# Column tiles side by side for the gate's low-rank product and for two routers' logits

## The reference, cut to what matters

```python
# block 1, mixer: the decay of gated linear attention comes from a product of rank 16
proj = n @ w_in                                   # glr is 16 of its columns
log_a = jax.nn.log_sigmoid((glr @ gla_gate_w2 + gla_gate_b).astype(jnp.float32)) / GLA_TAU   # (16, 256)
# block 1, router: 4 groups and 32 experts, 36 logits per token
g_logits = (x @ w_grp).astype(jnp.float32) + b_grp.astype(jnp.float32)
e_logits = ((x @ w_exp).astype(jnp.float32) + b_exp.astype(jnp.float32)).reshape(M, N_GROUPS, EXPERTS_PER_GROUP)
# block 2, router: each of 16 experts chooses 128 of the 1024 tokens by a softmax over 16 logits per token
```

## Time and profile before

| what | us |
|---|---|
| median of 3 runs (lowest, highest) | 3929.72 (3928.16, 3930.3) |
| span of the profiled execution, first to last instruction | 3925.4 |
| PE busy | 3703.1 (94%) |
| DVE busy | 2843.7 (72%) |
| ACT busy | 1858.2 (47%) |
| mean granted TensorE clock | 0.976 |

### The profile page before, as it was taken

How to read it: one execution, slowest core, us unless ns; L and a number is a source line. 1 busy time by engine, 2 the same in 40 slices (tenths; PEclk the granted TensorE clock), 3 DMA queues, 4 the chain that set the end, 5 groups by cost and what they waited for, 6 DMA issues and landing times. The chain is left out here.

```text
span 3925.4 us, 42186 instructions
## 1 busy us (share of the span) xinstructions
PE 3703.1 (94%) x16780; PEld 2848.1 (73%) x16780; DVE 2843.7 (72%) x2581; ACT 1858.2 (47%) x1720; POOL 264.7 (7%) x281
## 2 busy tenths in 40 slices
PE   8999998899999799999999989899499999999998
PEld 3557776788888677777887634578288888888886
DVE  2655455898988665556345899954799898888887
ACT  3243431778777334443011111211377777777776
POOL 0000000100000200000000000000000101010110
PEclk9999999899999899999999999999799999999999
DMA  3012024899998632223344515143699999999998
GB/s 119 6 51 83 17 93 188 317 419 415 415 415 335 241 116 68 68 67 104 95 123 151 201 56 187 54 161 129 225 373 386 382 389 382 388 381 389 385 385 318
DMA packets 367168, 891.04 MB, mean 227 GB/s; under 512 B 21994, under 2 KB 118609, under 8 KB 357556
## 3 DMA queue, kind: packets, MB, share of 16 engines
q1 hardware_dynamic: 323796, 758.12, 52.0%
q0 software_dynamic: 26896, 97.17, 7.0%
q10 hardware_dynamic: 16336, 33.82, 2.2%
HBM read 788.65 MB, written 100.40 MB: 226 GB/s over the span
## 5 line engine op out<-in xcount | busy, mean ns | idle before, releaser
L2346 DVE TENSOR_TENSOR moe_w_rest<-moe_w_w,moe_upper 128x2048 fp32r<-128x2048 f32 x384 | 862.3, 2288 | 131.9 <-ACT moe_upper L2255 70.7
L2247 ACT ACTIVATE moe_upper<-moe_w_w 128x2048 fp32r<-128x2048 f32 x192 | 357.4, 1909 | 225.0 <-PE moe_y_ps L2211 117.0
L2346 DVE TENSOR_TENSOR moe_w_rest<-moe_w_w,moe_upper_w 128x2048 fp32r<-128x2048 f32 x192 | 430.5, 2283 | 10.9 <-ACT moe_upper_w L2265 10.8
L2265 ACT ACTIVATE moe_upper_w<-moe_w_w 128x2048 fp32r<-128x2048 f32 x192 | 357.5, 1910 | 111.6 <-PE moe_up_ps L2185 81.3
L2255 ACT ACTIVATE moe_upper<-moe_w_w 128x2048 fp32r<-128x2048 f32 x192 | 356.7, 1911 | 0.2
L2185 PE MATMUL moe_up_ps<-moe_upper,moe_x_upper 128*128 128x512 f32 x768 | 308.4, 402 | 0.0
L2185 PE MATMUL moe_gate_ps<-moe_upper,moe_x_upper 128*128 128x512 f32 x768 | 300.8, 392 | 4.7 <-DVE moe_x_rest L2359 4.7
L2185 PE MATMUL moe_gate_ps<-moe_upper,moe_x_rest 128*128 128x512 f32 x768 | 300.3, 391 | 0.0
L2185 PE MATMUL moe_gate_ps<-moe_w_rest,moe_x_upper 128*128 128x512 f32 x768 | 300.1, 391 | 0.0
L2185 PE MATMUL moe_up_ps<-moe_upper,moe_x_rest 128*128 128x512 f32 x768 | 299.9, 390 | 0.0
L2185 PE MATMUL moe_up_ps<-moe_w_rest,moe_x_upper 128*128 128x512 f32 x768 | 298.9, 389 | 0.0
(11 more groups left out here) (636 smaller groups left out, 7512.2 us busy)
## 6 DMA issues: line engine op xcount, KB each, us to landing
moe_w_w<-in_expert_w_dram SPq DMA_DIRECT2D x96, 2048.0 KB, 10.8
moe_w_w<-in_w_gate_dram SPq DMA_DIRECT2D x64, 2048.0 KB, 10.8
moe_w_w<-in_w_up_dram SPq DMA_DIRECT2D x64, 2048.0 KB, 10.3
moe_w_w<-in_w_down_dram SPq DMA_DIRECT2D x64, 2048.0 KB, 10.3
tmp_y_rows<-moe_y ACTq DMA_DIRECT2D x32, 512.0 KB, 9.5
block_w_first<-in_w_in_dram SPq DMA_DIRECT2D x20, 512.0 KB, 3.8
tmp_h<-out_xn POOLq DMA_DIRECT2D x16, 512.0 KB, 3.0
tmp_spectra<-held_K ACTq DMA_DIRECT2D x8, 1024.0 KB, 4.7
```

What stands on the lines that cost most here:

```text
L2247: act.activation(half(upper1(c), h), half(weights.w1[c % 2], h), ACT.Copy).then_inc(m.w1_rounded, 1)
L2265: act.activation(half(upper2(i, c), h), half(weights.w2[c % 2], h), ACT.Copy).then_inc(m.w2_rounded, 1)
L2346: dve.tensor_tensor(half(rest, h), half(whole, h), half(upper, h).bitcast(F32), ALU.subtract).then_inc(done, 1)
```

## The change

1. The weights of each of the three products are padded with zeros to 32, 64 or 32 columns, and the 8 slices of the contraction are dealt to 4, 2 or 4 column tiles of TensorE. Matmuls of different slices write different partitions of one PSUM bank; each column tile accumulates its own 2 or 4 slices.
2. The partial sums are not added by an operation of their own. For the gate, `w2` is loaded 8 times, one copy below the other (7 DMAs more), so that "z" contracts over 128 rows where it contracted over 16 and sums as it multiplies. For the routers the transposes become matmuls with a small matrix of zeros and ones (`sums`, made from the identity by one DVE reduction), which turn and add at once.
3. The first half of the gate's product is computed after the fifth and sixth transpose (4 matmuls each), no longer in four parts.
4. The routers' logits are computed in three parts, tiles 0 to 3, 4 to 6 and 7 (`LOGIT_TILES`). In the first router part 0 stays ahead of the last transpose; in the second, parts 0 and 1 do. ACT copies what was made there between its last square root and its last tile copy.

```diff
+LOW_WIDTH = 2 * GLA_LOW
+LOW_SIDE = P // LOW_WIDTH
...
-        sp.dma_start(m.w2[:, :], m.gate_w2).then_inc(m.loaded["small"], 16)
+        for rows in range(P // GLA_LOW):
+            sp.dma_start(m.w2[bass.ts(rows, GLA_LOW), :], m.gate_w2).then_inc(m.loaded["small"], 16)
...
+    def pad_low(m, dve):
+        dve.memset(m.wlow[:, :, GLA_LOW:LOW_WIDTH], 0.0)
...
-        per = 2 * ND // NT
-        for k in range(per * part, per * (part + 1)):
-            last = m.nc.tensor.matmul(m.low_ps[0:GLA_LOW, 0, :], m.wlow[:, k, :], n_T[:, k, 0:BANK], start=(k == 0), stop=(k == ND - 1))
+        if part < ND // LOW_SIDE:
+            last = m.low_products(m.low_ps[:, 0, :], n_T, 0, part)
...
+    def low_products(m, out, n_T, h, r):
+        for g in range(LOW_SIDE):
+            k = r * LOW_SIDE + g
+            last = m.nc.tensor.matmul(out[bass.ts(g, LOW_WIDTH), :], m.wlow[:, k, :], n_T[:, k, bass.ts(h, BANK)],
+                                      start=(r == 0), stop=(r == ND // LOW_SIDE - 1))
...
+    def prepare(m, dve, ident):
+        dve.memset(m.w[:, :, m.n:m.width], 0.0)
+        dve.reduce_sum(m.sums[:, :], ident[:, :].rearrange("p (g n) -> p n g", n=m.width), axis=AXX)
+
+LOGIT_TILES = ((0, NT // 2), (NT // 2, NT - 1), (NT - 1, NT))
...
+def logit_parts(nc, pe, m, inputs, h_T, normed, part):
+    first_tile, last_tile = LOGIT_TILES[part]
+    cols = slice(first_tile * P, last_tile * P)
+    if part == 0:
+        pe.wait_ge(inputs.loaded, inputs.all_loaded)
+    pe.wait_ge(normed.copied, last_tile)
+    n_side = P // inputs.width
+    for r in range(ND // n_side):
+        for g in range(n_side):
+            k = r * n_side + g
+            last = nc.tensor.matmul(m.logit_T_ps[bass.ts(g, inputs.width), part, 0:(last_tile - first_tile) * P], inputs.w[:, k, :], h_T[:, k, cols],
+                                    start=(r == 0), stop=(r == ND // n_side - 1))
+    last.then_inc(m.logit_T_made, 1)
+
+def sum_logits(nc, pe, m, inputs, out, part):
+    pe.wait_ge(m.logit_T_copied, part + 1)
+    for t in range(*LOGIT_TILES[part]):
+        last = nc.tensor.matmul(out[:, t, :], m.logit_T[:, bass.ts(t, P)], inputs.sums[:, 0:inputs.n], start=True, stop=True)
...
-        router_logits(nc, pe, m, h_T, w, logit_ps, ident, logits_ready, [1])
+        logit_parts(nc, pe, m, inputs, h_T, normed, 1)
+        sum_logits(nc, pe, m, inputs, logit_ps, 0)
+        logit_parts(nc, pe, m, inputs, h_T, normed, 2)
+        for part in (1, 2):
+            last = sum_logits(nc, pe, m, inputs, logit_ps, part)
...
-        router_logits(nc, pe, m, h_T, w, logit_ps, ident, logits_ready, [1])
+        for part in (0, 1):
+            sum_logits(nc, pe, m, inputs, logit_ps, part)
+        logit_parts(nc, pe, m, inputs, h_T, normed, 2)
+        sum_logits(nc, pe, m, inputs, logit_ps, 2).then_inc(logits_ready, 1)
```

More of the change, by code:

```diff
@@ L371, in wait_stored, with residual_norm_phase @@
             engine.wait_ge(m.xn_stored[b], 16 * (NT // 2))
-def residual_norm_phase(nc, block, m, w, res, out, gain, ident, normed, normed_T, next_inputs, before_last_turn, act_made=None, in_blocks=False, n_rounded=AheadRows.N, n_rests=AheadRows.N):
+def residual_norm_phase(nc, block, m, w, res, out, gain, ident, normed, normed_T, next_inputs, before_last_turn, before_last_copy, act_made=None, in_blocks=False, n_rounded=AheadRows.N, n_rests=AheadRows.N):
     N_LATE = ND - m.n_ahead
@@ L467, in _ @@
                 split_act(t + 1)
+            if t == 1:
+                next_inputs.prepare(dve, ident)
             dve.wait_ge(prod_ready, t + 1)
@@ L712, in _ @@
                     if g == N_LOW:
-                        pe.wait_ge(w_loaded["small"], 48)
+                        pe.wait_ge(w_loaded["small"], SMALL_LOADED)
                         pe.wait_ge(low_ready, 2)
@@ L739, in _ @@
                         pe.wait_ge(w_loaded["r"], 16)
[L740 to L743, removed]
+                    for r in range(ND // LOW_SIDE if what == "low" else 0):
+                        last = inputs.low_products(out, n_T, h, r)
+                    for k in range(0 if what == "low" else ND):
+                        if what in "qk":
                             o, lhsT, rhs = out[:, :], wqk[:, k, bass.ds((what == "k") * GLA_QK + j * P, P)], n_T[:, k, bass.ts(h, BANK)]
@@ L795, in _ @@
         def _(act):
-            act.wait_ge(w_loaded["small"], 48)
+            act.wait_ge(w_loaded["small"], SMALL_LOADED)
             for g in range(N_LOW, N_Z):
@@ L1461, with __init__ @@
 class RouterInputs(Store):
-    def __init__(self, nc, name, ws, bs, rows="(k p) n -> p k n"):
+    def __init__(self, nc, name, ws, bs, width, rows="(k p) n -> p k n"):
         super().__init__(nc, name, side="right")
-        self.ws, self.bs, self.rows = ws, bs, rows
+        self.ws, self.bs, self.width, self.rows = ws, bs, width, rows
+        self.n = sum(w.shape[1] for w in ws)
     def open(m):
         super().open()
-        m.w = m.sb("w", [P, ND, sum(w.shape[1] for w in m.ws)])
+        m.w = m.sb("w", [P, ND, m.width])
+        m.sums = m.sb("sums", [P, m.width])
         m.bias = m.sb("bias", [P, max(1, sum(b.shape[0] for b in m.bs))])
@@ L1491, in add_logits @@
     m.logit_T_made = m.sem("logit_T_made")
     m.logit_T_copied = m.sem("logit_T_copied")
[L1495 to L1507, removed]
@@ L1510, in copy_logits @@
-def copy_logits(act, m):
-    for h in range(2):
-        act.wait_ge(m.logit_T_made, h + 1)
-        act.activation(m.logit_T[:, bass.ts(h, BANK)], m.logit_T_ps[:, bass.ts(h, BANK)], ACT.Copy).then_inc(m.logit_T_copied, 1)
+def logit_parts(nc, pe, m, inputs, h_T, normed, part):
[11 more added lines that the diff above has]
+    last.then_inc(m.logit_T_made, 1)
@@ new lines, in sum_logits, with copy_logits @@
+def sum_logits(nc, pe, m, inputs, out, part):
+    pe.wait_ge(m.logit_T_copied, part + 1)
+    for t in range(*LOGIT_TILES[part]):
+        last = nc.tensor.matmul(out[:, t, :], m.logit_T[:, bass.ts(t, P)], inputs.sums[:, 0:inputs.n], start=True, stop=True)
+    return last
+def copy_logits(act, m, part):
+    first_tile, last_tile = LOGIT_TILES[part]
+    cols = slice(first_tile * P, last_tile * P)
+    act.wait_ge(m.logit_T_made, part + 1)
+    act.activation(m.logit_T[:, cols], m.logit_T_ps[:, part, 0:(last_tile - first_tile) * P], ACT.Copy).then_inc(m.logit_T_copied, 1)
@@ L1645, in _ @@
     def _(act):
-        copy_logits(act, m)
+        copy_logits(act, m, 1)
+        copy_logits(act, m, 2)
         act.wait_ge(diff_ready, 1)
```

57 lines of the change are left out of this document (32 added, 25 removed).

## The result

The changed kernel takes 3945.63 us (median of 19 runs, 3940.78 to 3948.67) against 3928.16 before (19 runs, 3925.03 to 3954.77): ratio 1.004, 95% interval 1.0034 to 1.0047. It is 17.5 us slower; 22.9 us faster were forecast. The profiled spans are 3945.1 and 3925.4.

The account below looks back on a forecast made before the run. PE was taken as full in the gate's and experts' stages, so cuts ahead of them count in full: -8.6 - 4.9 - 9.4 = -22.9, span 3902.5, plus 4.3 to the median, 3906.8 us; range 3901 to 3915.

Parts of the forecast that it names:

- the part on what bounds the kernel: Gate's and experts' stages: PE busy throughout, no wait to fill, so time cut ahead of them arrives at the end in full.
- the sum: Whole kernel: gate and two routers together -22.9 us, a span of 3902.5, 3906.8 us as median.
- the experts' windows stay full: Sign of being right: in the changed profile PE stays busy throughout the experts' windows.
- the small loads: Rival at the gate: eight w2 issues of 6.35 us each delay wqk and q; +9.9 us, 3939.6; chance 4%.
- Gate, -8.6: Gate's low-rank product: column tiles and earlier second half start "z" at 29.95 instead of 38.67 us, -8.6 us.
- the clock: First q products: the lower clock level, costing 1.7 us, may go or move; counted 0, 2 us either way.
- Small loads of w2, cost 0: Gate: seven more w2 DMAs take 3.2 us of issue, yet wqk still arrives in time; cost 0.
- First router, -4.9: First router's logits: DVE starts at 665.2 instead of 670.09 us, -4.9 us.
- Second, -9.4: Second router's logits: DVE starts at 2754.1 instead of 2763.50 us, -9.4 us.
- Four column tiles at 1.8 us for 8 matmuls: Gate and second router: four column tiles over 128 rows run together, 8 matmuls in 1.8 us instead of 6.87.
- the first rival in the list: Two matmuls at a time, four tiles take 3.5 us: -6.0, -4.9, -7.0, together -17.9, 3911.8 us; chance 22%.

Follow-up runs that it names:

- e1: Changed kernel with 128 unused bytes a partition below each router's inputs: 3905.24 us, ratio 0.9942; run again, 3902.76 us, ratio 0.9931.
- e2: Kernel before with only unused bytes below its routers' inputs, 1152 B ahead of the first experts' weights, 640 B ahead of the second's: 3967.55 us, ratio 1.0097.
- e3: Kernel before with the gate's part of the change alone (column tiles for the low-rank product, gate_w2 loaded eight times): 3918.17 us, ratio 0.9973.
- g1: Changed kernel with e1's padding and 128 unused bytes ahead of the attention's own tiles as well: 3901.38 us, ratio 0.9929.
- k1: Kernel before with 128 unused bytes in the second experts between left-hand weight parts and what follows, moving the stationary tiles to 64 mod 256: 3950.25 us, single run.

## Why the prediction was wrong

**The step that failed** is in the part on what bounds the kernel. Of the gate's stage and the experts' it says: "Neither holds a wait that a shift could fill [...] So whatever is cut ahead of them arrives at the end in full." The experts' stages were read as fixed blocks, to be moved and not altered. That PE is full says the opposite of safe: with no idle time, each nanosecond of a matmul's pace goes into the total. The change alters that pace by where it puts tiles, and the sum had no term for it. The diff showed it: two tiles in the right-hand stack grow and two are new, ahead of the stack's largest users. A thing allocated there is part of the change just as a moved instruction is. The missing term is 40.7 us (14.17 + 1.87 + 24.66, the table above unrounded). e1 measured it as 40.4, or 42.2 with each kernel set against its own runs of the kernel before, and e2 as 37.6. One of the prediction's signs of being right was that "the experts' windows stay full": they did, and it said nothing of their pace. No rival held it: the one on the slow side (the small loads, 3939.6) ended 6 us below the measured time by another mechanism, and that mechanism did not occur.

**The terms, by their own steps:**
- Gate, -8.6 and "z" at 29.95: measured 29.84. (29.95 against 38.67 is 8.7, not 8.6.) q started 8.9 us earlier. At the last output product of block 1 the lead is 10.8; the rest fits the clock, which was granted in full from 43 to 47 us. It was counted 0 with 2 us either way. e3 puts the gate's part at 11.8 us in all, and in its trace the lead there is 12.1 (12.7 in e1). q's start (33.17) and the 1.7 us of the clock make 10.8 of e3's; for the rest there is only that the clock differs elsewhere too (280 to 400 us: 0.98 before, 1.00 in e3 and e1). So this term was sized some 3 us too small.
- Small loads of w2, cost 0: right; 9.56 us for eight, not eight times 6.35. That the queue "stood full" for the one long issue is the prediction's reading; no row shows what held it. In the rival on these loads, the landing at 66.5 lies 7.3 us behind the issue at 59.2, for which no row is given; with the 15.0 us of the earlier trace rows it would be 74.2.
- First router, -4.9: measured -4.92. Second, -9.4: measured -9.70.
- Four column tiles at 1.8 us for 8 matmuls: measured 1.92 for 16 records with the tail. The rule of strict program order that the prediction weighed, from the Trainium skill, "TensorE: Matmul & The Clock Gate", section "Packing small matmuls — row/col tiling", gave the size of the first rival in the list (the prediction calls it the second); the records show both passes of four tiles in that time, so they were not held one behind the other here. In what order the records of one bunch stand in the program can't be read from them.
- The sum: with the placement put right, 3905.24 and 3902.76 us were measured where 3906.8 was forecast. That it comes this close is in part luck. In e1's trace the gate and the two routers give 12.7, 4.7 and 9.4 us, which is 26.8 against the 22.9 of the sum, and 3.2 and 1.8 are lost between the blocks and in the second experts, for which the sum had no term either.

**What stays open.** The stretch from the first experts to the second output product grew by 4.2 us in the changed kernel, by 3.2 and 1.6 in the two traces of e1, by 3.8 in g1, and not at all in e2 and e3 (+0.1, -0.3). Set beside e3, e1 loses its part where the filters' spectra are made between the two blocks, and there the clock was lower for a few microseconds (0.66 of full speed over the 5 us from 1350, 1.00 in e3 in the same stage). For the changed kernel itself the windows there show the same mean clock as before (0.95 in 1330:1430), so this part is not explained. Nor are the 1.8 and 1.1 us by which the second experts last longer in e1's two traces than before, at the same 226.7 ns. And why the residues matter at all no run shows.

## What to carry to other kernels

Where PE is busy without a gap, read the distance between matmul starts too, and count it again after any change that resizes a tile, wherever the tile is used. Before a change to a tile's size is forecast, list the addresses of both versions and see which stages move: a few bytes a partition ahead of the largest tiles cost more here than three stages' good edits gave. Keeping the moving and the stationary tiles at one residue mod 256 costs less than 256 bytes a partition for each stack that has to be shifted, cheap enough to be tried first. Shown is this for fp32r tiles with matmuls of 128x512 alone; other types and shapes were not run.

## What the runs showed of the hardware

- The pace of 128x512 matmuls of fp32r tiles in a row depends on where the stationary and the moving tiles begin against each other: 226.7 ns with all at the same residue mod 256 (at 192 and at 64), 228.9 to 233.5 at six other differences, up to 3.0% more.
- The pace is lost by neighbours as well. In e2 only `w_o` moved in the second output product; yet the six products in a row that read `out_w`, which had not moved, slowed too. In the changed kernel:

```profile
2688.22 0.39 PE L431 MATMUL out_prod<-out_w_upper,out_act_upper 128*128 128x512 f32 x1
2688.45 0.40 PE L431 MATMUL out_prod<-out_w_rest,out_act_upper 128*128 128x512 f32 x1
2688.68 0.40 PE L431 MATMUL out_prod<-out_w_upper,out_act_rest 128*128 128x512 f32 x1
2688.92 0.40 PE L431 MATMUL out_prod<-out_w_upper,out_act_upper 128*128 128x512 f32 x1
2689.16 0.39 PE L431 MATMUL out_prod<-out_w_rest,out_act_upper 128*128 128x512 f32 x1
2689.38 0.39 PE L431 MATMUL out_prod<-out_w_upper,out_act_rest 128*128 128x512 f32 x1
```

  Five distances make 1.16 us; in e1 the same six starts lie 1.13 us apart (2694.30 to 2695.43). Why it is so is not shown, but it looks like the next point.
- At equal residues, too, the full pace comes only after some matmuls without a break. The second output product of the kernel before, all of whose tiles begin at 192, shows it at its start:

```profile
2654.78 0.40 PE L430 MATMUL out_prod<-w_o_w_upper,out_act_upper 128*128 128x512 f32 x1
...
2656.63 0.39 PE L430 MATMUL out_prod<-w_o_w_upper,out_act_rest 128*128 128x512 f32 x1
...
2658.90 0.39 PE L430 MATMUL out_prod<-w_o_w_upper,out_act_upper 128*128 128x512 f32 x1
```

  The eight distances from 2654.78 to 2656.63 make 1.85 us (231 ns each), the next ten 2.27 (227 each). In the experts' stages of before, the first nine distances after each break (a gap or other work) average 229.7 ns and the later ones 226.7. With `att_wv` at 64 the later ones stay at 232.5, and with it at 192 (g1) they come down to 226.7. The six products with `out_w` above follow products that never came down, and six may be too few to do so; no run tests this.
- The lower pace needs no contention with loads or with DVE. In e2 the same products ran 232 ns apart from 2698.67 to 2700.06 us (1.39 us for six), a stretch in which DVE had nothing to do and the DMA engines moved nothing. The window of it (columns as in the earlier trace rows):

```profile
2698.00:2700.06 2.06, 2.06 (x11) 1.62 (x10) 0.00 (x0) 0.00 (x0) 0.00 (x0) 1.00 0.00 0
```

  In the Trainium skill, "SBUF — State Buffer", section "SBUF: two separate sides", only the port pair shared by DVE and GpSimd causes contention and PE never waits on anyone. The slow pace without any such neighbour agrees with this. But "TensorE: Matmul & The Clock Gate", section "Step-by-step: what each phase is for", gives PE two independent read ports, one for the moving and one for the stationary operand. By that one would expect the two tiles' places not to matter to each other, and k1 shows that they do.
- Four column tiles of 128 rows and 32 columns run together in float32, with both passes: 16 records in 1.92 us, against 7.03 one after the other.
